# A decoder layer with a mixture of experts: the down bias moves to a product in the last stage, and the left rows' halves are added behind the rounding of the next weights

## The reference

```
logits = h2 @ router_w + router_b
top_v, top_i = top_k(logits, 4);  gates = softmax(top_v)
for every token and each of its four experts e:
    gu   = h2 @ w_gu[e] + b_gu[e]
    gate = min(gu[:1024], 7);  up = clip(gu[1024:], -7, 7)
    act  = (up + 1) * gate * sigmoid(1.702 * gate)
    y    = act @ w_down[e] + b_down[e]
    out += gates[e] * y
x = x + out
```

## Time and profile before

| | us |
|---|---|
| runs without profile (3) | 2579.34, 2579.87, 2588.82; median 2579.87 |
| profiled execution, its own time | 2585.97 |
| its span, first to last instruction | 2584.3 |
| TensorE busy / share | 2225.3 / 86% |
| DVE busy / share | 1617.1 / 63% |
| ACT busy / share | 1283.1 / 50% |
| mean granted TensorE clock | 0.917 of full |

### The profile page before, as it was taken

One profiled execution on the slowest core, in us unless ns is written; L12 is line 12 of the kernel. 1 busy time (PEld: TensorE's weight loads), 2 busy tenths in 40 slices (PEclk: granted clock), 3 DMA queues, 4 the chain that ended last, 5 costly groups with the idle time before them and its releaser, 6 DMA issues. The chain is left out here.

```text
span 2584.3 us, 38014 instructions
## 1 busy us (share of the span) xinstructions
PE 2225.3 (86%) x11995; PEld 1936.6 (75%) x11996; DVE 1617.1 (63%) x1973; ACT 1283.1 (50%) x1692; POOL 578.6 (22%) x610
## 2 busy tenths in 40 slices
PE   4899949598979429999999999999999999999960
PEld 3788837488868328897799889898777898788950
DVE  4320037474542526787866786786788867887746
ACT  4121124253432025666765675666676666766640
POOL 1430014331210241122211131121232311322114
PEclk9999979585789659999999999999999999999985
DMA  4122130322333166799987798796999978999768
GB/s 141 45 107 100 59 94 21 71 62 66 115 125 115 63 178 221 252 304 302 358 288 232 252 346 271 252 303 228 323 357 362 361 244 269 356 318 300 258 201 363
DMA packets 453456, 560.97 MB, mean 217 GB/s; under 512 B 62804, under 2 KB 342357, under 8 KB 453397
## 3 DMA queue, kind: packets, MB, share of 16 engines
q1 hardware_dynamic: 440373, 517.46, 61.2%
q0 software_dynamic: 13024, 42.75, 4.7%
HBM read 504.73 MB, written 55.35 MB: 217 GB/s over the span
## 5 line engine op out<-in xcount | busy, mean ns | idle before, releaser
L1511 DVE TENSOR_TENSOR VL<-RAW,VH 128x2048 fp32r<-128x2048 f32 x389 | 887.7, 2287 | 152.5 <-ACT VH L1506 149.7
L1506 ACT ACTIVATE VH<-RAW 128x2048 fp32r<-128x2048 f32 x390 | 725.9, 1907 | 110.3 <-DMA RAW<-in_expert_w_gate_up 70.3
L1909 PE MATMUL banks<-T,VH 128*128 128x384 f32 x1920 | 551.0, 361 | 19.0 <-DVE yb L1812 7.9
L1911 PE MATMUL banks<-T,VL 128*128 128x192 f32 x1680 | 422.5, 251 | 0.0
L1909 PEld LDWEIGHTS banks<-T,VH 128*128 128x128 f32 x1920 | 355.2, 189 | 25.1 <-issue 25.1
L1911 PEld LDWEIGHTS banks<-T,VL 128*128 128x128 f32 x1680 | 323.0, 192 | 0.0
L167 PE MATMUL banks<-VH,T 128*128 128x512 f32 x544 | 212.4, 391 | 0.0
L166 PE MATMUL banks<-VL,T 128*128 128x512 f32 x544 | 212.4, 390 | 0.0
L165 PE MATMUL banks<-VH,T 128*128 128x512 f32 x544 | 212.0, 390 | 0.0
L165 PE MATMUL banks<-VH,A 128*128 128x512 f32 x512 | 202.1, 395 | 5.2 <-DVE A L1749 5.1
L167 PE MATMUL banks<-VH,A 128*128 128x512 f32 x512 | 200.5, 392 | 0.0
(11 more groups left out here) (319 smaller groups left out, 4197.4 us busy)
## 6 DMA issues: line engine op xcount, KB each, us to landing
RAW<-in_expert_w_gate_up SPq DMA_DIRECT2D x264, 1024.0 KB
RAW<-in_expert_w_down SPq DMA_DIRECT2D x130, 1024.0 KB
dY<-yb SPq DMA_DIRECT2D x98, 128.0 KB
RAW<-in_w_in SPq DMA_DIRECT2D x6, 2048.0 KB, 8.6
dY<-zeros SPq DMA_DIRECT2D x17, 512.0 KB, 6.0
dY<-yb SPq DMA_DIRECT2D x32, 256.0 KB
xin<-in_x SPq DMA_DIRECT2D x8, 512.0 KB
qks<-dK SPq DMA_DIRECT2D x16, 256.0 KB
```

What stands on the lines that cost most here:

```text
L1506: act.activation(VH[:, i, ks], RAW[:, i, ks], ACT.Copy).then_inc(s_hi, 1)
L1511: dve.tensor_tensor(VL[:, i, ks], RAW[:, i, ks], VH[:, i, ks].bitcast(f32), ALU.subtract).then_inc(s_w, 1)
L1909: last = pe.matmul(o[:, 0:2 * NW], VH[:, c % 3, k, col], T2[:, k], start=k == 0, stop=k == KT - 1)
L1911: pe.matmul(o[:, HI_ALL], VL[:, c % 3, k, col], T2[:, k, HI_ALL], start=False, stop=False)
```

## The change

- `bias_in` and the btab table keep the gate and up biases only (two chunks a row group instead of three). The products with the down bias are gone: c = 4 and 5 of narrow blocks, c = 4 and 5 of wide blocks, and L1930 in the left rows. The down products open their own sum.
- s_bu is raised earlier: at the bias product of c = 3 in narrow blocks, at the last VL product of the eighth column tile in wide ones. hot_e takes another place in SBUF.
- In wide down chunks ACT's fold stands behind `round_next`, and DVE's left add behind `first_half`. The 128 rows go to yb with the chunk's parity, the left rows to a buffer of their own, yl, with the chunk's parity; the store semaphores go by chunk.
- Stage 5 computes G, the gates spread over 32 experts for each token, in two more DVE operations, and loads and splits a smaller table.
- Stage 7 loads b_dn three times, splits G and b_dn into parts, turns G (8 transposes), multiplies (2 products of 512 columns a token tile, 96 rows deep) and adds the result from PSUM to acc in one more DVE operation a tile, ahead of the four.

The core of the diff (indentation shortened):

```diff
+    link(dve.tensor_tensor(g4[:], g4[:], bc(gsum[:].unsqueeze(2), [P, TT, TOPK]), ALU.mult))
+    link(dve.tensor_tensor(prod[:], sel[:], bc(g4[:].rearrange("p t k -> p (t k)").unsqueeze(2), [P, TT * TOPK, NE]), ALU.mult))
+    dve.tensor_reduce(G[:], prod[:].rearrange("p (t k) e -> p t e k", k=TOPK), X, ALU.add)
...
-                    sp.dma_start(dY[bass.ds(fb * UN + h * P, height(h)), (c - GU) * CH:(c - GU + 1) * CH], yb[0:height(h), h]).then_inc(s_st[h], 16)
+                    sp.dma_start(dY[bass.ds(fb * UN + h * P, height(h)), (c - GU) * CH:(c - GU + 1) * CH], (yb[:, c % 2], yl[0:UN, c % 2])[h]).then_inc(s_st[c % 2], 16)
...
         for c in range(GU, NCH):
             tokens_hi(c - GU, s * 2 + (c - GU + 3))
             act.wait_ge(s_mm, s * N2 + (2 * c + 1))
-            act.wait_ge(s_st[0], s * 32 + (32 if c > GU else 16))
-            act.activation(yb[:, 0], ps[2 * (c % 2)], ACT.Copy).then_inc(s_ea, 1)
-            act.wait_ge(s_mm, s * N2 + (2 * c + 2))
+            act.wait_ge(s_st[c % 2], s * 32 + 16)
+            act.activation(yb[:, c % 2], ps[2 * (c % 2)], ACT.Copy).then_inc(s_ea, 1)
+            round_next(s, c)
             act.wait_ge(s_yl, s * 2 + (c - GU + 2))
             act.activation(yfold, ps[2 * (c % 2) + 1][UN:2 * UN], ACT.Copy).then_inc(s_ea, 1)
-            round_next(s, c)
...
         for c in range(GU, NCH):
             tokens_lo(c - GU, s * 2 + (c - GU + 3))
             second_half(s, c)
+            first_half(s, c)
             dve.wait_ge(s_ea, s * N2 + (2 * c + 6))
-            dve.wait_ge(s_st[1], s * 32 + (32 if c > GU else 16))
-            dve.tensor_tensor(yb[0:UN, 1], ps[2 * (c % 2) + 1][0:UN], yfold, ALU.add).then_inc(s_yl, 1)
-            first_half(s, c)
+            dve.wait_ge(s_st[c % 2], s * 32 + 16)
+            dve.tensor_tensor(yl[0:UN, c % 2], ps[2 * (c % 2) + 1][0:UN], yfold, ALU.add).then_inc(s_yl, 1)
...
-            last = mm3(pe, o, left[:, k, HI[0]], left[:, k, LO[0]], VH[:, c % 3, k], VL[:, c % 3, k], False, k == KT - 1)
+            last = mm3(pe, o, left[:, k, HI[0]], left[:, k, LO[0]], VH[:, c % 3, k], VL[:, c % 3, k], c >= GU and k == 0, k == KT - 1)
...
+    def bias_in(o, c):
+        return pe.matmul(o, hot_e[:, c // 2], btab[:, (c % 2) * CH:(c % 2 + 1) * CH], start=True, stop=False)
...
-            biased = bias_in(o, c, P)
             if c < GU:
+                biased = bias_in(o, c)
+                if c == GU - 1:
+                    biased.then_inc(s_bu, 1)
                 product(s, o, c, T2, range(KT)).then_inc(s_mm, 2)
...
             else:
-                biased.then_inc(s_bu, 1)
...
-                        pe.matmul(o[:, HI_ALL], VL[:, c % 3, k, col], T2[:, k, HI_ALL], start=False, stop=False)
+                        used = pe.matmul(o[:, HI_ALL], VL[:, c % 3, k, col], T2[:, k, HI_ALL], start=False, stop=False)
...
+            if i == G2 - 1:
+                used.then_inc(s_bu, 1)
...
-            bias_in(o, c, P)
...
-            left_product(o, c, range(KT - 1))
-            biased = pe.matmul(o[0:UN], hot_e[:, c // 3, 0:UN], btab[:, (c % 3) * CH:(c % 3 + 1) * CH], start=False, stop=False)
-            if c == NCH - 1:
-                biased.then_inc(s_bu, 1)
-            left_product(o, c, [KT - 1]).then_inc(s_mm, 1)
+            left_product(o, c, range(KT)).then_inc(s_mm, 1)
...
+    for g in range(3):
+        sp.dma_start(bdr[NE * g:NE * g + NE], b_dn).then_inc(s_bd, 16)
...
+    act.wait_ge(s_gT, 1)
+    act.activation(GT[0:3 * NE], pair(3, S)[0:3 * NE], ACT.Copy).then_inc(s_gt, 1)
+
+@block.tensor
+def _(pe):
+    pe.wait_ge(s_g3, 3)
+    for t in range(TT):
+        last = pe.transpose(pair(3, S)[0:3 * NE, tok(t)], G3[:, t].bitcast(f32), ident[:])
+    last.then_inc(s_gT, 1)
+    pe.wait_ge(s_gt, 1)
+    pe.wait_ge(s_blo, 1)
+    for t in range(TT):
+        if t >= 3:
+            pe.wait_ge(s_xb, t - 2)
+        for j in range(2):
+            last = pe.matmul(ps[2 * (t % 3) + j], GT[0:3 * NE, tok(t)], bd3[0:3 * NE, j * CH:(j + 1) * CH], start=True, stop=True)
+        last.then_inc(s_yb, 1)
+
 @block.vector
 def _(dve):
+    dve.tensor_copy(G3[:, :, 0:NE], G[:]).then_inc(s_g3, 1)
+    dve.wait_ge(s_g3, 1)
+    dve.tensor_copy(G3[:, :, 2 * NE:3 * NE], G3[:, :, 0:NE].bitcast(f32)).then_inc(s_g3, 1)
+    dve.tensor_tensor(G3[:, :, NE:2 * NE], G[:], G3[:, :, 0:NE].bitcast(f32), ALU.subtract).then_inc(s_g3, 1)
+    dve.wait_ge(s_bhi, 1)
+    low = slice(2 * NE, 3 * NE)
+    dve.tensor_tensor(bd3[low], bdr[low], bd3[low].bitcast(f32), ALU.subtract).then_inc(s_blo, 1)
     for t in range(TT):
         dve.wait_ge(s_x[t % 2], 16 * (t // 2 + 1))
+        dve.wait_ge(s_yb, t + 1)
+        dve.tensor_tensor(acc[:, t], acc[:, t], pair(t % 3, D), ALU.add).then_inc(s_xb, 1)
+        dve.wait_ge(s_xb, t + 1)
         dve.wait_ge(s_k[t % YR], 16 * TOPK * (t // YR + 1))
         for k in range(TOPK):
             dve.scalar_tensor_tensor(out=acc[:, t], in0=yk[:, t % YR, k], scalar=g4[:, t, k:k + 1], in1=acc[:, t],
```

More of the change, by code:

```diff
@@ L83, in layer_kernel @@
     ident = ext.take("ident", [P, P])
+    A_CONST = ext.at
     ones = ext.take("ones", [P, P])
@@ L1276, in layer_kernel @@
     tokr = r5.take("tokr", [P, P])
-    braw = r5.take("braw", [P, 3 * CH])
+    braw = r5.take("braw", [P, 2 * CH])
+    G = Region(A_CONST + 2 * P * 4, KB).take("G", [P, TT, NE])
     diag = r5.take("diag", [P, SSB + 1])
@@ L1292, in _ @@
                 for g in range(4):
-                    for j in range(3):
-                        sp.dma_start(bias_rows(braw[32 * g:32 * g + NE], j, j + 3 * (g // 2)), bias_of(j + 3 * (g // 2))).then_inc(s_braw, 16)
+                    for j in range(2):
+                        sp.dma_start(bias_rows(braw[32 * g:32 * g + NE], j), bias_of(j + 2 * (g // 2))).then_inc(s_braw, 16)
                 sp.wait_ge(s_tab, 1)
@@ L1397, in _ @@
                     dve.tensor_scalar(rowkey[32 * g:32 * g + NE, g // 2:g // 2 + 1], srow[32 * g:32 * g + NE], -32.0 * g, None, ALU.add)
-                dve.wait_ge(s_braw, 16 * 12)
-                up = braw[0:64].rearrange("p (j g n) -> p j g n", j=3, g=2)[:, :, 1]
+                dve.wait_ge(s_braw, 16 * 8)
+                up = braw[:].rearrange("p (j g n) -> p j g n", j=2, g=2)[:, :, 1]
                 dve.tensor_scalar(up, up, 1.0, None, ALU.add).then_inc(s_bt, 1)
-                up = braw[64:128, HC:CH]
-                dve.tensor_scalar(up, up, 1.0, None, ALU.add).then_inc(s_bt, 1)
+                dve.wait_ge(s_bt, 1)
+                dve.tensor_copy(btab[:], braw[:]).then_inc(s_bt, 1)
                 dve.wait_ge(s_bt, 2)
-                dve.tensor_copy(btab[:], braw[:]).then_inc(s_bt, 1)
-                dve.wait_ge(s_bt, 3)
                 for at in (32, 96):
@@ L1413, in _ @@
                 dve.wait_ge(s_bT, 1)
-                for q, n in ((0, 6), (1, 2)):
-                    dve.tensor_copy(btT[:, :, 6 * q:6 * q + n], ps[4 + q][:, 0:2 * n * NE].rearrange("p (g i e) -> p g i e", g=2, i=n))
+                for q in range(2):
+                    dve.tensor_copy(btT[:, :, 4 * q:4 * q + 4], ps[4 + q][:, 0:8 * NE].rearrange("p (g i e) -> p g i e", g=2, i=4))
                 dve.wait_ge(s_e, 1)
@@ L1437, in _ @@
                 pe.matmul(ps[3][:, 0:SSB + 1], ones[:], diag[:], start=True, stop=True).then_inc(s_exp, 1)
-                pe.wait_ge(s_bt, 2)
+                pe.wait_ge(s_bt, 1)
                 for g in range(2):
@@ L1441, in _ @@
                         c, j = i // 2, i % 2
-                        rows, at = slice(64 * (c // 3), 64 * (c // 3) + NE), (c % 3) * CH + g * HC + j * P
-                        q, n = c // 3, 6 - 4 * (c // 3)
-                        last = pe.transpose(ps[4 + q][:, (g * n + i % 6) * NE:(g * n + i % 6 + 1) * NE], braw[rows, at:at + P], ident[rows, rows])
+                        rows, at = slice(64 * (c // 2), 64 * (c // 2) + NE), (c % 2) * CH + g * HC + j * P
+                        last = pe.transpose(ps[4 + c // 2][:, (4 * g + i % 4) * NE:(4 * g + i % 4 + 1) * NE], braw[rows, at:at + P], ident[rows, rows])
                 last.then_inc(s_bT, 1)
@@ L1463, in layer_kernel @@
     yb = r6e.take("yb", [P, 2, CH])
-    btab = r6e.take("btab", [P, 3 * CH], f32r)
-    hot_e = r6e.take("hot_e", [P, 2, P], f32r)
+    yl = r6e.take("yl", [P, 2, CH])
+    btab = r6e.take("btab", [P, 2 * CH], f32r)
+    hot_e = Region(A_CONST, KB).take("hot_e", [P, 2, P], f32r)
     r6t = Region(A_TR, 4 * KB)
@@ L1493, in bias_of, with bias_rows @@
     def bias_of(c):
[L1495 to L1502, removed]
+        return b_gu.rearrange("e (g n) -> e g n", g=2)[:, :, c * HC:(c + 1) * HC]
+    def bias_rows(rows, j):
+        return rows[:, j * CH:(j + 1) * CH].rearrange("p (g n) -> p g n", g=2)
     def split_hi(act, i, hf):
@@ L1848, in left_product @@
                     return last
-                def bias_in(o, c, m):
-                    return pe.matmul(o, hot_e[:, c // 3, 0:m], btab[:, (c % 3) * CH:(c % 3 + 1) * CH], start=True, stop=False)
```

(21 more changed lines are left out.)

1 line of the change is left out of this document (removed).

## The result

The changed kernel takes 2548.16 us (median of 4 runs, 2544.90 to 2550.86) against 2579.61 for the kernel before (4 runs, 2572.61 to 2588.82). The ratio is 0.9875, with a 95% interval of 0.9842 to 0.9909. The forecast of 2560.3 was a ratio of 0.9924, and the low end of its range, 2549.0, lies 0.8 above what was measured.

A forecast was written before the change was run, and what follows sets the result against it. TensorE was taken to bound the expert stage except in narrow runs, where transfers set the pace. Terms - 13.8 - 6.0 - 5.4 + 3.3 + 2.3 = - 19.6 gave 2560.3 us; range 2549 to 2573 for 8 in 10.

The forecast's parts named there:

- Wide products: In wide blocks TensorE is the pace, so four products fewer in each of 15 take 13.8 us off.
- Wide to wide: At wide-to-wide block ends, the earlier one-hot gains 1.0 us net of a late left sum; six ends, 6.0.
- End of the expert stage: After the last block, the later left add delays SP's empty rounds; cost 3.3 us, nothing hides it.
- the narrow runs at zero: Narrow runs of two, three, three and six blocks: transfers no earlier or later, so no gain counted.
- rival B: Transfers leave room in narrow runs, being queued late rather than slow; 10 us more gain, 2550; chance 0.12.
- Lone narrow blocks: Three single narrow blocks each gain 1.8 us from the earlier start, bias product and one-hot; 5.4 in all.
- First end: The very first wide-to-wide block end, where TensorE also waits for its loop's return; left as it is.
- Last stage: DVE's added bias sum makes it the bound by 0.3 us a tile; with bias loads, 2.3 us cost.
- Stage 5: Stage before the experts: extra DVE work falls into its idle time behind the token scatter; zero cost.
- C: Late left sum eats all that the one-hot gives at block ends; gain 8.2 us, 2571.7; chance 0.17.
- D: The last stage hides none of its adds; 9 us more, 2569; chance 0.07.
- E: In wide blocks the one-hot, started first, delays DVE's last low halves; 37 us slower, 2597; chance 0.04.

The follow-up runs named there:

- e5: Changed kernel with one more product at four places in each wide block's down chunks, 60 in all, results overwritten; 2566.07 us, one run.
- e2: Changed kernel with the left rows' fold ahead of ACT's rounding and the add before DVE's first low half again; 2547.37 us, ratio 0.9874.
- e1_after: The changed kernel itself, measured once more against the kernel before; 2551.24 us, ratio 0.9889.
- e3_late_hot: Changed kernel with the one-hot released as late as before the change, in narrow and wide blocks; 2565.23 us, ratio 0.9937.
- e4: Changed kernel with one more product in each down chunk of every narrow block, 34 in all, results overwritten; 2562.97 us, ratio 0.9912.
- e7: e2 with TensorE also adding dX1 to the bias product in the last stage, DVE's separate add gone; 2539.68 us, ratio 0.9864.

## Why the prediction was right and wrong

**Right, with the size.** *Wide products*: forecast 13.8, and e5 gives back 13.7 for the same number of products. *Wide to wide*: forecast 1.0 at each of six ends through a sum that makes tile two 0.65 late. By the rows above, 1.75 is off the pause and 0.76 given back, so 1.0. The blocks themselves, from T to T, went from 59.13 to 59.29 before to 57.34 to 57.41 after; without the 0.92 of the products that leaves 0.9, 5.4 in all. e2 takes the late tile away and finds wide after wide at 56.43. *End of the expert stage*: forecast 3.3, measured 3.5. SP's empty rounds now run later than DVE's, where before they ran earlier; source line L1541 of the kernel after, durations in ns, first and last start:

```profile
L1541 DVEq ALU_OP  x22: 40/40/40, 2453.3 to 2467.7; - x22
...
L1541 SPq ALU_OP  x22: 32/33/36, 2454.8 to 2468.6; - x22
```

In e2, with the early sum, it is 19.3, against 19.5 before.

**Wrong: the narrow runs at zero.** The step that failed reads "So the transfers are no earlier and no later, and a run bound by them ends where it did". It went from a true row (DMA share 1.06 over the run) to a conclusion about its beginning. The prediction had even noted that the load at T+17.1 stood behind TensorE's second chunk, and then took the load as bound by the transfer before it, through by T+16.6. It had moved the first load to T+10.6 (right: 10.5) but not the second, which goes with TensorE: it came at T+15.4, before the first had arrived, and queued behind it. In e1_after, whose trace has the landings, the first load was complete at T+18.6 and the second at T+24.6; in e3_late_hot at T+19.2 and T+25.6. The pause of 1.56 that the change removes is thus a gain of 1.9 to 2.3 in the runs of two, three, three and six as well: 8.2 in all, where none was counted. With it the forecast would have been 2552.1. The sign that the prediction had set for this step, a run of six still about 230 with a DMA share over 1, came true (229.5, 1.07) and didn't test it: the length of a run doesn't say when it begins. The same error made rival B unlikely. B had the sign right (narrow blocks gain too) and the place (late issue, not slow transfer), and its 2550 was near, but its sum was not what happened: it gave the 14 further blocks 0.33 each, 4.6, for the products and the one-hot, and e4 shows that all 34 products in narrow blocks are worth 1.6 to 2.0.

**Mis-sized.** *Lone narrow blocks*: 1.8 forecast, 1.9 to 2.0 measured. *First end*: taken as unchanged, but the first two blocks together give back 1.8 of the 1.84 that the sum gives them for products. TensorE's pause there was 3.78 before, 4.75 after and up to 5.09 in the other runs of the changed code with an early one-hot. Behind the pause the granted clock is at its lower level, 1.2 GHz. Here a stretch inside each of those times, the kernel before and then the one after (columns as in rows 1):

```profile
1020.50:1023.80 3.30, 3.30 (x13) 3.30 (x14) 1.61 (x1) 1.18 (x2) 2.50 (x2) 0.50 0.93 344
```

```profile
1005.20:1011.90 6.70, 6.22 (x23) 6.23 (x24) 1.07 (x2) 0.57 (x2) 0.00 (x0) 0.50 0.75 277
```

It lasted 3.4 us before and 6.8 in all eight runs of changed code. So TensorE worked 2.9 us longer at half the clock, by estimate 1.5 lost, beside 1.0 of the longer pause. In the first block the clock was back at full 4.7 us after the start instead of 5.7, by estimate 0.5 gained. Together that is 2.0, about the 1.8 that is missing. Why the pause is longer wasn't tried.

*Last stage*: 2.3 forecast; 1.3 to 2.3 measured, in six executions. The distance of 6.6 between tiles was 6.54. *Stage 5*: forecast zero, 0.9 and 1.1 measured; e2 and e7 took 86.5 and 86.3 there with the same code as e1 in stage 5, so the figure isn't the change's alone. The eight executions of the changed stage took 86.3 to 89.3, and the spread is there already when SP loads the token table behind the token scatter, 67.3 to 70.1 us into the stage.

The terms as measured, -31.7 + 0.9 + 3.5 + 1.5 = -25.8, make a ratio of 0.9900 by the profiled executions. That lies inside both intervals. Taken from 2579.87 they give 2554.1, inside the stated range, so the terms alone don't bring the time below it. What the medians show beyond them (-31.4 in the first comparison, -26.8 in e1_after) can't be told from the draw of the clock in stages 1 to 4.

**The rivals.** C (nothing left of the one-hot's gain) falls: taking the early one-hot away costs 17.2 (e3). D (no add hidden) falls: the add costs 0.24 of its 1.22 a tile. E (the one-hot keeps DVE from the last low halves) did not happen, though the two do meet. Timeline of the kernel after at the end of a gate and up phase:

```profile
1369.43 1.05 POOL L1622 TENSOR_SCALAR hot_e<-rowkey,ecur 128x256 fp32r<-128x256 f32 x1 [0.21 <-POOL ecur L1620]
1369.46 0.63 DVE L1753 SCALAR_TENSOR_TENSOR A<-qa,A 128x128 fp32r<-128x128 f32 x2 [0.43 <-ACT A L1671]
```

The one-hot starts 0.03 ahead; the pair of low halves takes 0.63 instead of 0.43, and the one-hot 1.05. So 0.2 us of a slack of over 2 is used, and a wide block after a narrow one takes 56.2 to 56.3 from its first product to T whether the one-hot is early (after) or late (e3_late_hot). The rule of the Trainium skill that was weighed in the prediction (SBUF — State Buffer, Who interferes with whom: the two lock each other out for a whole instruction) isn't what this row shows in full, since both instructions run at once for 0.6 us by the profile, whose times for POOL are rough; the measurement decides, and the order here costs nothing.

## What to carry to other kernels

A high DMA share over a stretch says that transfers set its length, not when it begins: follow the first few issues of the stretch one by one, and ask of each what released it. If that is the engine which the change makes earlier, the whole stretch moves with it. And a step that is moved behind another takes its waiters along: here the late sum cost about 5.5 inside the expert stage and 3.7 at its end, and moving it back kept every other gain.

## What the runs showed of the hardware

- The same code of stages 1 to 4 took from 853.7 to 884.0 us in nine profiled executions, one of each run here, with granted clocks of 0.59 to 0.78 in the same two 100 us windows, while the expert stage, at 1.00 but for its first blocks, took 1505.9 to 1507.8 in three executions of the same code. One execution each is no base for a difference of 10 us in the whole time.
- A multiply-add on DVE whose second input lies in PSUM took 1.28 us for 128x1024, no longer than one whose inputs lie in SBUF (5.25 for four, 1.31 each), so an addend can be left there for it.
- The one-hot on POOL took 4.95 where it met two of DVE's splits in a row, 2.9 to 3.0 where it met one, and 1.05 beside the pair of low halves; with one split it ended 0.8 behind the split's end. Every split kept its 2.28 to 2.29, so POOL paid. Source line L1622 of the kernel after, 33 times, durations min, median and max in ns:

```profile
L1622 POOL TENSOR_SCALAR hot_e<-rowkey,ecur x33: 947/2935/2997, 931.9 to 2431.7; 128x256 fp32r<-128x256 f32 x33
```
